# Trips of h through scratch memory on ScalarE's queue, with chunk 0's trip in two halves, in an encoder trunk on one Trainium2 core

## The reference

```python
for l in range(DEPTH):
    x = x + 0.5 * _swiglu(_rmsnorm(x, ffn1_norm[l]), ffn1_w_in[l], ffn1_w_out[l])
    h = _rmsnorm(x, mix_norm[l])
    ...      # spatial gating and windowed attention on h @ w_mix_in[l]
    x = x + jnp.concatenate([out_a, out_b], axis=-1) @ w_mix_out[l]
    x = x + 0.5 * _swiglu(_rmsnorm(x, ffn2_norm[l]), ffn2_w_in[l], ffn2_w_out[l])
# _swiglu(h, w_in, w_out): gate, up = split(h @ w_in);  (silu(gate) * up) @ w_out
```

## Time and profile before

| | |
|---|---|
| median of three runs | 916.62 us |
| the profiled execution's own time | 915.78 us |
| its span, first to last instruction | 914.0 us |
| TensorE busy | 895.2 us (98%) |
| VectorE busy | 561.6 us (61%) |
| ScalarE busy | 448.2 us (49%) |
| GpSimd busy | 56.0 us (6%) |
| mean granted TensorE clock | 0.993 |
| moved by DMA | 190.05 MB, 63.0% of the DMA engines' time on SP's queue |

### The profile page before, as it was taken

The page is one execution under the profiler, slowest core; times in us unless marked ns, Lnnn a source line. Parts: engine busy times, 40 slices in busy tenths (PEclk is TensorE's granted clock), DMA queues, the critical chain, the costliest instruction groups (busy, mean ns, idle before and its releaser), DMA issues.

```text
span 914.0 us, 12202 instructions
## 1 busy us (share of the span) xinstructions
PE 895.2 (98%) x4230; PEld 736.3 (81%) x4230; DVE 561.6 (61%) x758; ACT 448.2 (49%) x522; POOL 56.0 (6%) x115
## 2 busy tenths in 40 slices
PE   8699999999999999999999999999999999999998
PEld 7488888888778788888887888888877878888887
DVE  5464655657977555555566565555779666565562
ACT  5444434447856354444444544444578454354340
POOL 3400000103100000000020000000111000000000
PEclk9899999999999999999999999999999999999999
DMA  8678877854265687767637777676433757687731
GB/s 281 190 253 237 258 215 251 247 196 138 94 207 168 225 263 224 261 205 236 215 106 248 250 234 264 218 240 192 136 134 117 252 160 255 218 261 234 251 138 47
DMA packets 150722, 190.05 MB, mean 208 GB/s; under 512 B 9268, under 2 KB 124280, under 8 KB 150688
## 3 DMA queue, kind: packets, MB, share of 16 engines
q1 hardware_dynamic: 149216, 186.55, 63.0%
q0 software_dynamic: 1296, 2.92, 1.4%
q10 hardware_dynamic: 176, 0.14, 0.0%
HBM read 176.72 MB, written 12.84 MB: 207 GB/s over the span
## 4 chain that ended last, share of the span: by engine, by line
PE 85%; DVE 6%; DMA 4%; ACT 3%; SPq 1%; issue 1%; POOL 0%; ACTq 0%; DVEq 0%; POOLq 0%
PE U L1148 10%; PE U L1151 10%; PE U L1149 10%; PE TR L1151 6%; PE TR L1149 6%; PE TR L1148 6%; PE C L1148 6%; PE C L1151 6%; PE C L1149 6%; PE D L1148 5%; PE D L1149 5%; PE D L1151 5%; DMA h_rows<-qs 2%; DVE w_lo L792 2%; DVE sc L997 1%
## 5 line engine op out<-in xcount | busy, mean ns | idle before, releaser
L792 DVE TENSOR_TENSOR w_lo<-raw,w_hi 128x2048 fp32r<-128x2048 f32 x150 | 340.8, 2287 | 98.0 <-ACT w_hi L556 97.5
L556 ACT ACTIVATE w_hi<-raw 128x2048 fp32r<-128x2048 f32 x150 | 283.6, 1908 | 43.7 <-DMA raw<-in_ffn_w_in_dram 37.5
L1148 PE MATMUL U<-w_hi,xT 128*128 128x512 f32 (+1 forms) x448 | 172.9, 386 | 0.0
L1151 PE MATMUL U<-w_hi,xT 128*128 128x512 f32 (+1 forms) x448 | 171.1, 382 | 0.0
L1149 PE MATMUL U<-w_lo,xT 128*128 128x512 f32 (+1 forms) x448 | 171.1, 382 | 0.0
L586 ACT ACTIVATE hT_hi<-gv 128x256 fp32r<-128x256 f32 x80 | 29.0, 410 | 199.8 <-DMA gv<-h_rows 199.8
L1148 PE MATMUL TR<-w_hi,xT 128*128 128x512 f32 x320 | 124.6, 389 | 0.0
L1151 PE MATMUL TR<-w_hi,xT 128*128 128x512 f32 x320 | 124.5, 389 | 0.0
L1149 PE MATMUL TR<-w_lo,xT 128*128 128x512 f32 x320 | 124.5, 389 | 0.0
L829 DVE TENSOR_TENSOR hT_lo<-gv,hT_hi 128x256 fp32r<-128x256 f32 x80 | 30.4, 422 | 114.0 <-ACT hT_hi L586 114.0
L1148 PEld LDWEIGHTS U<-w_hi,xT 128*128 128x128 f32 x448 | 84.2, 188 | 16.5
(11 more groups left out here) (160 smaller groups left out, 974.3 us busy)
## 6 DMA issues: line engine op xcount, KB each, us to landing
raw<-in_ffn_w_in_dram SPq DMA_DIRECT2D x168, 512.0 KB, 5.5
raw<-in_ffn_w_out_dram SPq DMA_DIRECT2D x88, 512.0 KB, 4.2
raw<-in_w_mix_in_dram SPq DMA_DIRECT2D x28, 512.0 KB, 4.7
h_rows<-qs SPq DMA_DIRECT2D x40, 256.0 KB, 4.0
gv<-h_rows SPq DMA_DIRECT2D x160, 64.0 KB, 1.9
raw<-in_w_mix_out_dram SPq DMA_DIRECT2D x16, 512.0 KB, 3.7
raw<-in_ffn_w_in_dram SPq DMA_DIRECT2D x16, 256.0 KB, 4.7
bias<-bias_rows POOLq DMA_DIRECT2D x8, 192.0 KB, 3.9
```

The source lines that it names most:

```text
L556: act.activation(w_hi[:, p % SLOTS, :], raw[:, p % RAW, :], ACT.Copy).then_inc(hi_ready, 1)
L792: dve.tensor_tensor(w_lo[:, p % SLOTS, :], raw[:, p % RAW, :], w_hi[:, p % SLOTS, :].bitcast(F32), ALU.subtract).then_inc(lo_ready, 1)
L1148: pe.matmul(out_, x_hi, w_hi[:, slot, c], start=start, stop=False, skip_group_check=reopened)
L1151: last = pe.matmul(out_, x_lo, w_hi[:, slot, c], start=False, stop=stop, skip_group_check=reopened)
```

## The change

`store_h` and `load_h` move from SP's program to ScalarE's. SP's FFN program keeps weights only; three loads (the key and value part of w_mix_in and the first units of the next layer) keep their order. On ScalarE, `store_h(c)` stands at the end of `chunk(c)`, behind the split of w_out, and `load_h(c-1)` at the head of `chunk(c)`, ahead of the first split. Chunk 0's trip is cut by token tile: each tile is turned, stored (128 KB, to its own scratch), loaded (four DMAs of 32 KB, pieces of 64 floats) and rounded by itself, with semaphores of its own, and TensorE leaves tile 0 when tile 0's rest is there. Every chunk from 1 to 9 takes the same single trip as before, from the other queue.

```diff
-            def store_h(L, f, c, j=0):          # SyncE
-                sp.wait_ge(h_turned, n_turned(L, f, c, j))
-                sp.dma_start(h_rows, h_turns).then_inc(h_stored, 16)
...
             def ffn_weights(L, f):              # SyncE
                 def chunk(c, j=0):
                     load_in(L, f, c + 1, 0, j)
                     load_in(L, f, c + 1, 1, j)
-                    store_h(L, f, c - 1, j)
-                    load_h(L, f, c - 1, j)
                     load_out(L, f, c, j)
...
+            def store_h0(L, f, t):              # ScalarE
+                act.wait_ge(h_turned, n_turned(L, f, 0, t))
+                act.dma_start(h_rows_0[t], h_turns[:, t * FC:(t + 1) * FC]).then_inc(h0_stored[t], 16)
+            def load_h0(L, f, t):
+                act.wait_ge(h0_stored[t], 16 * (2 * L + f + 1))
+                for g in range(4):
+                    src = bass.AP(h_rows_0.tensor, t * P * FC + g * 64, [[FC, 32], [32 * FC, 4], [1, 64]])
+                    act.dma_start(h_cols[32 * g:32 * g + 32, t * FC:(t + 1) * FC]..., src).then_inc(h0_loaded[t], 16)
+            def round_h0(L, f, t):
+                act.wait_ge(h0_loaded[t], 64 * (2 * L + f + 1))
+                act.activation(h0_as_tokens(hT_hi, t), h0_as_loaded(h_cols, t), ACT.Copy).then_inc(hT_hi_done, 1)
...
                 def chunk(c, j=0):              # ScalarE
-                    split(L, pos_in(f, c + 1, 0), j)
-                    round_h(L, f, c - 1, j)
+                    if c == 1:
+                        load_h0(L, f, 1)
+                        round_h0(L, f, 0)
+                        split(L, pos_in(f, 2, 0))
+                        round_h0(L, f, 1)
+                    else:
+                        load_h(L, f, c - 1, j)
+                        split(L, pos_in(f, c + 1, 0), j)
+                        round_h(L, f, c - 1, j)
                     split(L, pos_in(f, c + 1, 1), j)
                     silu(L, f, c, 0, j)
                     silu(L, f, c, 1, j)
                     split(L, pos_out(f, c), j)
+                    store_h(L, f, c, j)
...
                 if L == 0 and f == 0:
                     sum_squares(0, -1, 1)
+                    store_h0(L, f, 0)
                     silu(L, f, 0, 1)
                     split(L, pos_in(f, 1, 1))
+                    store_h0(L, f, 1)
+                    load_h0(L, f, 0)
+                    split(L, pos_out(f, 0))
                 else:
                     split(L, pos_in(f, 1, 1))
+                    store_h0(L, f, 0)
                     silu(L, f, 0, 1)
-                split(L, pos_out(f, 0))
+                    split(L, pos_out(f, 0))
+                    store_h0(L, f, 1)
+                    load_h0(L, f, 0)
...
+            def turn_h0(L, f, t):               # VectorE
+                dve.wait_ge(h_done, n_ffn(L, f, 0, t))
+                cols = slice(t * FC, (t + 1) * FC)
+                dve.transpose(h_turns[:, cols], h_blocks[:, cols]).then_inc(h_turned, 1)
...
                 def chunk(c, j=0):              # VectorE; the copy of the gains now stands ahead of this
+                    if c == 1:
+                        rest_h0(L, f, 0)
+                        rest_h0(L, f, 1)
+                        split(L, pos_in(f, 2, 0))
+                    else:
+                        split(L, pos_in(f, c + 1, 0), j)
+                        rest_h(L, f, c - 1, j)
...
                 def leave(c, t, j=0, stop=False):   # TensorE
-                    pe.wait_ge(hT_lo_done, n_ffn(L, f, c, t if c == 10 else 1, j))
+                    pe.wait_ge(hT_lo_done, n_ffn(L, f, c, t if c in (0, 10) else 1, j))
```

More of the change, by code:

```diff
@@ L89, in h_as_tokens, with h0_as_loaded, h0_as_tokens @@
     return v.rearrange("p (t i n) -> p t i n", t=2, i=4)
+def h0_as_loaded(v, t):
+    return v.rearrange("p (t i k n) -> p t k i n", i=4, t=2, k=2)[:, t, :, :, :]
+def h0_as_tokens(v, t):
+    return v[:, 0, :, t * P:(t + 1) * P].rearrange("p k (i n) -> p k i n", n=32)
 def runs_of_buckets():
@@ L310, in n_gu, with n_turned, n_trip @@
             return L * (2 * NCH) + j * 2 + (NCH * f + c + 1)
-        def n_turned(L, f, c, j=0):
-            return L * (2 * (NCH - 1)) + j * 2 + ((NCH - 1) * f + c + 1)
+        def n_turned(L, f, c, t=0, j=0):
+            return L * (2 * NCH) + j * 2 + (NCH * f + (t + 1 if c == 0 else c + 2))
+        def n_trip(L, f, c, j=0):
+            return L * (2 * (NCH - 2)) + j * 2 + ((NCH - 2) * f + c)
         def n_hT(L, f, t):
@@ L399, in load_a, with ffn_weights @@
                                  ).then_inc(a_loaded[t], 16)
-            def store_h(L, f, c, j=0):
-                sp.wait_ge(h_turned, n_turned(L, f, c, j))
-                sp.dma_start(h_rows, h_turns).then_inc(h_stored, 16)
-            def load_h(L, f, c, j=0):
-                sp.wait_ge(h_stored, 16 * n_turned(L, f, c, j))
-                for g in range(4):
-                    src = bass.AP(h_rows.tensor, g * P, [[2 * FC, 32], [32 * 2 * FC, 4], [1, P]])
-                    sp.dma_start(h_cols[32 * g:32 * g + 32, :].rearrange("p (i n) -> p i n", i=4), src
-                                 ).then_inc(h_loaded, 16)
-            def ffn_weights(L, f, after):
+            def ffn_weights(L, f):
                 def chunk(c, j=0):
@@ L418, in chunk @@
                     load_in(L, f, c + 1, 1, j)
-                    store_h(L, f, c - 1, j)
-                    load_h(L, f, c - 1, j)
                     load_out(L, f, c, j)
-                load_in(L, f, 1, 0)
-                load_in(L, f, 1, 1)
-                load_out(L, f, 0)
+                chunk(0)
                 with sp.Fori(0, 4) as j:
@@ L429, in ffn_weights @@
                 load_out(L, f, 10)
-                if after is not None:
-                    after()
-                store_h(L, f, 9)
-                load_h(L, f, 9)
             sp.dma_start(xs[:, 0, :], x_tiles[0]).then_inc(x_loaded[0], 16)
@@ L453, in _ @@
                 load_in(L, 1, 0, 1)
-                ffn_weights(L, 1, (lambda: load_first(L + 1, 0)) if L < DEPTH - 1 else None)
+                ffn_weights(L, 1)
                 if L < DEPTH - 1:
-                    load_first(L + 1, 1)
+                    for u in range(2):
+                        load_first(L + 1, u)
             for t, half in ((0, 0), (0, 1), (1, 0)):
@@ L587, in round_h @@
                                    ).then_inc(hT_hi_done, 1)
+            def store_h0(L, f, t):
[3 more added lines that the diff above has]
+                act.wait_ge(h0_stored[t], 16 * (2 * L + f + 1))
+                for g in range(4):
+                    src = bass.AP(h_rows_0.tensor, t * P * FC + g * 64, [[FC, 32], [32 * FC, 4], [1, 64]])
+                    act.dma_start(h_cols[32 * g:32 * g + 32, t * FC:(t + 1) * FC].rearrange("p (i n) -> p i n", i=4), src
+                                  ).then_inc(h0_loaded[t], 16)
+            def round_h0(L, f, t):
+                act.wait_ge(h0_loaded[t], 64 * (2 * L + f + 1))
+                act.activation(h0_as_tokens(hT_hi, t), h0_as_loaded(h_cols, t), ACT.Copy).then_inc(hT_hi_done, 1)
             def sum_squares(L, ph, t):
@@ L824, in turn_h, with rest_h0 @@
                 dve.transpose(h_turns, h_blocks).then_inc(h_turned, 1)
+            def turn_h0(L, f, t):
+                dve.wait_ge(h_done, n_ffn(L, f, 0, t))
+                cols = slice(t * FC, (t + 1) * FC)
+                dve.transpose(h_turns[:, cols], h_blocks[:, cols]).then_inc(h_turned, 1)
+            def rest_h0(L, f, t):
+                dve.wait_ge(hT_hi_done, n_ffn(L, f, 0, t))
+                dve.tensor_tensor(h0_as_tokens(hT_lo, t), h0_as_loaded(h_cols, t), h0_as_tokens(hT_hi, t).bitcast(F32),
+                                  ALU.subtract).then_inc(hT_lo_done, 1)
             def rest_h(L, f, c, j=0):
@@ L903, in chunk @@
                 def chunk(c, j=0):
-                    split(L, pos_in(f, c + 1, 0), j)
-                    rest_h(L, f, c - 1, j)
                     if L == 0 and f == 0 and c == 1:
```

26 lines of the change are left out of this document (21 added, 5 removed).

## The result

| | before | after |
|---|---|---|
| median of the runs (lowest to highest), us | 917.42 (914.06 to 919.45) | 954.44 (952.32 to 956.84) |
| ratio to before, 95% interval | | 1.0408 (1.0367 to 1.0449) |
| profiled execution: own time, span, us | 915.78, 914.0 | 954.68, 952.9 |
| mean granted clock | 0.993 | 0.982 |

Both columns are of four runs, taken side by side. The change makes the kernel 4.1% slower, and the predicted range (896 to 909 us) does not hold the time. I read the page of after first: the busy times, the chain by engine, the chain by line, then the median landings of its trips, whole ones and chunk 0's halves.

What follows compares the result with a forecast made beforehand. TensorE bounds the kernel, busy 895.2 of 914.0 us, so only its stalls at chunk 0 can be won. 915.8 less 11.8 - 1.0 + 5.8 = 16.6 gives 899.2, against the median 900 us; range 896 to 909.

Steps and rivals of the forecast that it cites:

- the 18.6 us: TensorE's losses at chunk 0's leaving in the four FFNs, 12.9 us of them waits: all that the change can win.
- the other 36 trips: Trips of chunks 1 to 9 in the four FFNs: claimed to make TensorE wait nowhere.
- Part 3: Trips of chunks 1 to 9 on ScalarE: rests end at 155.5, 4 us of slack left, costed at nothing.
- The landings: Stores and loads of h: old medians and maxima used; 4.0 us taken for chunk 0's half store, 3 for its loads.
- Parts 1 and 2: Chunk 0's leaving: first FFN wins 11.8 us less 1.0 put back, the other three 6.7 - 0.9 = 5.8 us.
- Rival B: First FFN, chunk 0: bias store catches tile 1's loads, 5.5 us stand, lower clock; 908, milder 903 to 908; chance 0.17.
- rival C: Blocked ScalarE brings chunk 1's splits or chunk 2's w_in late: 3 to 4 us per FFN, 912 to 917; chance 0.09.
- Rival D: Chunks 1 to 9: ScalarE's landing wait delays rests over 4 us beyond reckoning; one us beyond gives 936; chance 0.06.

Runs made afterwards that it cites:

- e6: Before with the bias store held back, chunk 0's trip ahead of the second w_in load, chunk 1's products and turn ahead of the second split; 910.62 us.
- e9: e6 plus, in chunk 2, SyncE storing h(1) ahead of both w_in loads of chunk 3 and loading it ahead of the second; 901.70 us.
- e10: e9 with GpSimd's bias store back at its place in before; 902.60 us, ratio 0.9856.
- e4: Before with each trip's h loads issued as eight of 32 KB in place of four of 64, still on SyncE's queue; 956.45 us.
- e3: After with both w_in splits ahead of h's loads and round, and their rests ahead of h's rest, from chunk 2 on; 943.84 us.
- e7: After with one wait added: SyncE issues w_out's unit only when h's loads have landed; 934.72 us, ratio 1.0188.
- e8: e3 with chunk 1's products and turn ahead of the second split and rest, w_in's first rest between h's two rests; 941.74 us.
- e11: After with, in chunk 2 only, the round and rest of h(1) ahead of the split and rest of w_in's first unit; 962.29 us.
- e12: e11 with SyncE's w_in loads of chunk 3 held until h(1)'s store has landed; 965.42 us, ratio 1.0524.
- e1: Before with only after's chunk 0 (two halves on ScalarE's queue), trips of chunks 1 to 9 left on SyncE's queue; 922.44 us, ratio 1.0083.
- e2: Before with all ten trips of an FFN moved to ScalarE's queue, chunk 0's left whole; 943.25 us, ratio 1.0273.
- e5: Before with GpSimd's store of the bias rows held back until TensorE has used four of the FFN's units; 914.28 us, ratio 0.9987.

## Why the prediction was wrong

**What bounds the kernel, and the 18.6 us.** Right. e6, e9 and e10 win 18.5 to 18.6 us at chunk 0, step for step as the earlier trace rows gave them (11.8, 3.7, 1.1, 1.9). All that the stalls cost, the lower clock after them included, comes back together. That the other 36 trips make TensorE wait nowhere was true of waits and false of slack: no wait in a trace does not say how near the next one is.

**Part 3 is the step that failed.** The prediction put the rests at 155.5 and went on: "TensorE wants them at 159.55. So 4 us of slack are left, and I cost the part at nothing." That compares one chunk's rest with one chunk's want and follows a delay forward to TensorE alone. It leaves out the way back: behind the round stand the split of w_in's second unit and its rest, and behind these the products, the turn, the next store and the next trip. (The split that I had moved 4.9 us, to 150.5-152.4, is the first unit's. In after's chunk it ended at 160.14, and the round waited 2.43 us more for the loads, so it did not lengthen that loop.) Slack of a closed loop is the period less the loop's length, 16.3 less 14.9 to 15.7, about 1 us. e4 measured it (1.8 us more costs 30 us behind chunk 0), e3 agrees from the other side (loop opened and stores quicker, loss in chunks 2 to 10 gone). The longer landings took more than that: in the chunk shown the loop is 17.84 us. Chunks 2 to 10 lost 22.2 us, where the prediction had nothing.

**The landings.** This is the second step that failed, and it is what filled the slack. I used the old medians and maxima, and read the Trainium skill's sentence on shared engines as "landings stay as they are". That the engines are the same does not make the traffic on them the same. In before SyncE could not issue w_out's unit until the loads were issued; its serial list had shielded the trip. Freed from the trip it sent weights beside it: loads went from 1.9 to 3.3 us, stores from 4.0 to 5.1. I had seen the effect ("that traffic can meet the loads of h") and put no price on it. e7 puts a price on w_out's unit beside the loads: 20 us between the medians. Between the profiled executions it is 16.7 us, 12.3 of them in chunks 2 to 10. Why the stores became slower no run separates; that they need not be slow on ScalarE's queue is shown by e3 and e8, where the median is 2.0 us.

**Parts 1 and 2, chunk 0.** The direction was right, the size not: I put 1.0 us back of 11.8 and 0.9 of 6.7; after put back 3.1 and 4.4. The half trips were not quicker than a whole one (store 5.2, loads 3.7 with pieces of 256 B, against 4.0 and 1.9), so the rests of tile 0 ended at 33.68 as reckoned to within 1.2 us, but tile 1's at 38.47 for the 34 to 36 of the prediction, and the second FFN won nothing. The half turn took 0.45 us for my 0.36, and the half rounds and rests 0.42 each for 0.4; those were harmless. In the second FFN tile 0's products are done 3.6 us before the turn (291.67 and 295.30 in the earlier trace rows), and not "over 4 us". Half of the run-to-run spread is 2 us, so the range should have read 895 to 910. Neither changes the outcome.

**Rival B** happened, in a way that it had not foreseen. It asked whether tile 1's loads come so late that they meet the bias store at 32.83. They came early (the issues begin at 28.10), and the bias store came earlier still. GpSimd's timeline in after, then ScalarE's issues for tile 1:

```profile
21.67 6.08 POOL L511 COPY brow<-rb 8x38 f32<-8x38 f32 x31
28.05 0.74 POOL L516 DMA_DIRECT2D bias_rows<-brow  x1 [0.30 <-POOL brow L511]
```

```profile
28.10 4.67 ACTq L610 DMA_DIRECT2D gv<-h_rows  x4
```

So the store left at 28.05, 4.8 us before its time in the earlier trace rows, and four issues took 4.67 us where I had taken 1.8. The longest of these issues took 3.3 us. Its signs were the ones that the prediction gave for B: issues over 1 us beside the bias store, and a second leaving (bank D, 1.8 us) that waits. I had taken the bias store's time as fixed; it was not: the copies ahead of it ended 4.8 us sooner.

**Chunk 1 had no term in the sum; it was in the working only in rival C ("brings chunk 1's splits or w_in of chunk 2 late"), at 3 to 4 us in each FFN.** It cost 4.9 to 8.4, in sum 28.7, and was the largest term. Two things were not followed. First, a chunk 0 that no longer stands means that TensorE wants h(1) earlier by all that was won, while ScalarE and VectorE have had no time given to them. Second, the turn of h(1) stands behind both w_in rests, and its store goes out right behind 2 MB of weights. e9 takes away both causes (the products and turn ahead of the second rest, the store ahead of the loads) and chunk 1 loses nothing, but on before's queue and with whole trips; no run does it in after itself. e8, e11 and e12, each of which mends one thing in after's order, lose elsewhere what they win. e1 shows that 17.2 of it come even when h(1) travels on SyncE's queue.

**Rival D** named the right mechanism and side: "ScalarE's wait for the landing takes the place of SP's in the loop". Its price was "one us beyond gives 936". Its signs are there: eleven waits for `hT_lo`, 27.7 us in sum, and a clock of 0.982 for 0.993. The threshold was wrong: it was to decide once the rests come over 4 us later, and really about 1 us was enough. So it got a chance of 0.06, which a slack of 1 us would have raised well above that. What lengthened the loop was not the wait on ScalarE as such but the landings. The 954 us are D's loss and chunk 1's together, which no rival had.

**What stays open.** Chunks 9 and 10 lost 12.5 us in after and 13.7 in e2, where TensorE waits at line 1339 for the last products, which stand behind a late w_out rest and the late h(9). e3 and e1 have none of this, so it goes with the loop, but no run took it alone. The 5.8 us that e9 still loses arise at chunk 2 of the first FFN: h(2)'s store is issued at 55.57, right behind four w_in loads (46.61 to 55.43), and lands after 8.9 us; no run moved it. And I did not separate how much of a store's landing is its own write and how much is weights; e12 gives only the two ends.

## What to carry to other kernels

Before moving a step, write down the ring that it belongs to, from an event to the same event one period later, through every engine, and compare its length with the period; the slack is the difference. The time by which one result comes before it is wanted is what that slack has saved up over the chunks before, and a loop that is too long uses it up. The trace shows that length wherever an engine is catching up after a stall: take its intervals there, and not in the steady state, where the bottleneck paces them. And ask what a queue's serial order keeps apart: an engine that no longer waits will issue its large transfers sooner, beside the small ones whose landing someone waits for, and a stall removed at one chunk brings forward what the next one wants.

## What the runs showed of the hardware

- The landing of a 256 KB store depends on what is in flight, and not on which queue issued it: for h(1) of the first FFN 2.7 us with w_in held back (e12), 3.7 us ahead of the loads (e9), 5.2 us in their midst (e8), 7.0 us ahead of them but beside GpSimd's store (e10), 7.4 us behind 2 MB of w_in on ScalarE's queue (after), 8.6 us behind them on SyncE's own (e1). The medians of the 36 whole stores on ScalarE's queue are 5.1 us in after and 2.0 us in e3 and e8, where both splits stand ahead of the loads of h.
- Halving a store to 128 KB did not shorten its landing: median 5.2 us against 5.1 of the whole ones at other places of the same kernel. Loads of 32 KB in pieces of 256 B took 3.7 us against 3.3 of 64 KB (in e7, 2.3 against 2.0).
- Four load issues took 1.76 us, and 5.70 us beside a store of GpSimd's from 8 partitions; moving that store away (e5) brought back 1.76, and the issues that then ran beside it took 4.82 us.
- GpSimd's 31 small copies ahead of the bias store took 6.08 us in after, where VectorE is busy for 3.23 us of that stretch (53%), 10.24 us in before (7.90 us, 77%) and 10.70 us in e10 (9.21 us, 86%). That VectorE slows them is my reading; no run changed it alone.
- ScalarE's DMA issues do not wait for the end of the operation ahead of them. In after, timeline of ScalarE in the second FFN:

```profile
304.95 1.91 ACT L554 ACTIVATE w_hi<-raw 128x2048 fp32r<-128x2048 f32 x1
306.50 0.35 ACTq L603 DMA_DIRECT2D h_rows<-qs  x1
```

The store is issued at 306.50, and the split that stands ahead of it runs until 306.86. It is a small help for a trip on that queue, and no help to what stands behind the trip's waits.
